# Gate one-hot rows for eight tokens at once, 72 candidate sums a head, and index look-ups in f16 in a decoder step with product-key experts

## The reference

```python
s1 = einsum('nhd,hkd->nhk', q[..., :half], sk[:, 0])      # 8 heads, 128 keys in each half
s2 = einsum('nhd,hkd->nhk', q[..., half:], sk[:, 1])
v1, i1 = top_k(s1, 16);  v2, i2 = top_k(s2, 16)
cand = (v1[..., :, None] + v2[..., None, :]).reshape(n, 8, 256)
cidx = (i1[..., :, None] * 128 + i2[..., None, :]).reshape(n, 8, 256)
sv, si = top_k(cand, 16)
e = take_along_axis(cidx, si);  g = softmax(sv)           # 128 experts and gates a token
y[n] = sum over hk of g[n, hk] * gelu(x[n] . u[e[n, hk]]) * v[e[n, hk]]
```

## Time and profile before

| | |
|---|---|
| time, median of 3 runs | 3537.03 us (3536.31 to 3539.16) |
| the profiled execution | 3537.08 us |
| span of its profile | 3535.3 us (1.8 us lie around it) |
| TensorE busy | 3286.6 us, 93% |
| VectorE busy | 2575.6 us, 73% |
| ScalarE busy | 1313.2 us, 37% |
| GpSimd busy | 1025.6 us, 29% |
| first and last matmul of `product` start | 1211.9 and 2428.0 us |

### The profile page before, as it was taken

How to read it: one execution, slowest core, us unless ns; L and a number is a source line. 1 busy time by engine, 2 the same in 40 slices (tenths; PEclk the granted TensorE clock), 3 DMA queues, 4 the chain that set the end, 5 groups by cost and what they waited for, 6 DMA issues and landing times. The chain is left out here.

```text
span 3535.3 us, 54538 instructions
## 1 busy us (share of the span) xinstructions
PE 3286.6 (93%) x20435; PEld 1984.8 (56%) x20435; DVE 2575.6 (73%) x5334; ACT 1313.2 (37%) x2581; POOL 1025.6 (29%) x1074
## 2 busy tenths in 40 slices
PE   7999988599889897999999999996999999999997
PEld 4668652366366554556565655653555555555554
DVE  4222651354423499999999999986888888888887
ACT  3000651221210123567767766662222222222222
POOL 0000000000000003699989988972111111111110
PEclk9999999788899998999999999998999999999998
DMA  3220875512422343878788787889878878888874
GB/s 144 95 95 31 310 280 217 188 72 105 182 64 76 115 178 131 248 256 280 271 286 286 271 290 258 282 294 405 303 284 303 293 285 296 299 288 294 296 285 153
DMA packets 213105, 803.41 MB, mean 227 GB/s; under 512 B 33825, under 2 KB 92321, under 8 KB 169089
## 3 DMA queue, kind: packets, MB, share of 16 engines
q1 hardware_dynamic: 176000, 531.81, 41.5%
q0 software_dynamic: 36864, 268.45, 21.7%
HBM read 665.19 MB, written 201.98 MB: 245 GB/s over the span
## 5 line engine op out<-in xcount | busy, mean ns | idle before, releaser
L1669 PE MATMUL psum<-arena 128*128 128x400 f16 x6144 | 1098.5, 337 | 45.4 <-DVE arena L1717 45.0
L2026 PE MATMUL psum<-arena 128*128 128x400 f16 x6144 | 1050.2, 332 | 26.9 <-DVE arena L2072 26.9
L2026 PEld LDWEIGHTS psum<-arena 128*128 128x128 f16 x6144 | 596.7, 97 | 480.4 <-DVE arena L2072 27.3
L1669 PEld LDWEIGHTS psum<-arena 128*128 128x128 f16 x6144 | 598.5, 99 | 474.1 <-DVE arena L1717 53.4
L1641 POOL TENSOR_SCALAR arena<-arena 128x128 f16<-128x128 f16 x800 | 711.9, 903 | 52.6 <-DVEq L1847 26.1
L116 POOL DMA_INDIRECT arena<-in_experts,arena x256 | 301.7, 1179 | 1180.8 <-DVE arena L149 1081.9
L135 ACT ACTIVATE arena<-arena 128x1 f32<-128x1 f32 x256 | 51.6, 202 | 920.2 <-DVE arena L128 920.1
L149 DVE SCALAR_TENSOR_TENSOR arena<-arena 128x1024 f32<-128x1024 f32 x256 | 330.9, 1293 | 21.3 <-ACT arena L139 5.2
L2079 DVE TENSOR_TENSOR arena<-arena,psum 128x800 f32<-128x800 f32 x256 | 252.0, 984 | 108.7 <-PE psum L2026 108.7
L128 DVE CUSTOM_DVE_ANT_0 arena<-arena 128x1024 f32<-128x1024 f32 x256 | 311.4, 1219 | 13.3 <-DMA arena<-in_experts,arena 12.3
L1898 ACT ACTIVATE arena<-arena 128x128 f16<-128x128 f16 x800 | 245.1, 388 | 89.2 <-DVE arena L1855 89.0
(11 more groups left out here) (230 smaller groups left out, 3569.2 us busy)
## 6 DMA issues: line engine op xcount, KB each, us to landing
arena<-in_u_feat SPq DMA_DIRECT2D x128, 512.0 KB, 6.8
arena<-in_experts SPq DMA_DIRECT2D x128, 512.0 KB, 5.4
scratch_acts<-arena SPq DMA_DIRECT2D x128, 400.0 KB, 4.4
arena<-scratch_gates SPq DMA_DIRECT2D x32, 1600.0 KB, 8.0
arena<-scratch_acts SPq DMA_DIRECT2D x128, 400.0 KB, 6.7
scratch_gates<-arena SPq DMA_DIRECT2D x48, 1024.0 KB, 6.7
out_k_win_sample<-in_cache_k SPq DMA_DIRECT2D x32, 1022.0 KB, 21.7
out_v_win_sample<-in_cache_v SPq DMA_DIRECT2D x32, 1022.0 KB, 21.7
```

The lines of the kernel that those rows point to most:

```text
L1669: last = pe.matmul(psum[:, 2 * p + k, 0:SLD], w[:, s, q, :], xs[:, q, k * SLD:(k + 1) * SLD], start=q == 0 and w is u_hi and xs is x_hi, s ...
L2026: last = pe.matmul(psum[:, 2 * (n % BANKS) + i, 0:SLD], w[:, s, k, q * P:(q + 1) * P], hs[:, s, k, i * SLD:(i + 1) * SLD], start=k == 0 an ...
```

## The change

- The one-hot rows of a unit are made for eight tokens at once with tokens innermost (`hots[partition, kind, key, token]`, f16): VectorE makes two instructions of 128x1024 (second index, then first index), both `is_equal` of a constant table `expert8` against the f16 indices of the eight tokens. GpSimd multiplies the second by the gate's high and low part, two `tensor_tensor` of 128x1024. ScalarE's `low_hots` is gone. The matmuls read single tokens out of this, so that both operands step by eight f16 elements.
- `copy_picks` is two copies and subtractions with f16 outputs instead of seven instructions.
- Of the 256 sums a head only 72 are made, in four blocks; `places_to_parts` finds the two parts of a place in them with some 14 small instructions in place of three.
- `one_hot` and `select_indices` work on f16 with the 16 candidates outermost; the two reductions become four additions of halves each (`collect`).
- At the stage's start GpSimd makes two tables of 1024 and 2048 elements in place of one of 128; VectorE waits for them.
- The semaphores follow: GpSimd's rows wait for VectorE's (`second_hots_ready`), TensorE waits for GpSimd's and VectorE's (`hots_ready`, `first_hots_ready`), VectorE also for GpSimd's rows of two units before.

```diff
+PAIR_BLOCKS = ((0, 2, 16, 0), (2, 2, 8, 32), (4, 4, 4, 48), (8, 8, 1, 64))
+NPAIR = 72
...
-            pool.iota(iota_i, pattern=[[1, P]], base=0, channel_multiplier=0).then_inc(iota_ready, 1)
-            pool.wait_ge(iota_ready, 1)
-            pool.tensor_copy(iota, iota_i).then_inc(iota_ready, 1)
-            pool.wait_ge(iota_ready, 2)
+            pool.iota(count8, pattern=[[1, P], [0, 8]], base=0, channel_multiplier=0).then_inc(iota_ready, 1)
+            pool.iota(count16, pattern=[[1, 16], [0, P]], base=0, channel_multiplier=0).then_inc(iota_ready, 1)
+            pool.wait_ge(iota_ready, 2)
+            pool.tensor_copy(expert8, count8).then_inc(iota_ready, 1)
+            pool.tensor_copy(j16, count16).then_inc(iota_ready, 1)
+            pool.wait_ge(iota_ready, 4)
...
-            def first_hots(unit):
+            def gate_hots(unit):
+                pool.wait_ge(second_hots_ready, unit["group"] // 2 + 1)
                 if unit["before"] > 0:
                     pool.wait_ge(gates_ready, unit["before"])
                 pool.wait_ge(picks_copied, order[unit["tile"]] + 1)
                 turned = turned_picks[:, order[unit["tile"]] % 2]
-                for i in range(4 * unit["groups"]):
...
-                    last = pool.tensor_scalar(hots[:, unit["buffer"], i, 0, :], iota, turned[:, 0, token:token + 1], None,
-                                              ALU.is_equal)
+                for k in range(2):
+                    some = turned[:, 2 + k, unit["token"]:unit["token"] + 8]
+                    last = pool.tensor_tensor(hots[:, unit["buffer"], 2 + k], hots[:, unit["buffer"], 1],
+                                              some.unsqueeze(1).broadcast_to([P, P, 8]), ALU.mult)
+                last.then_inc(hots_ready, 1)
...
-                pe.wait_ge(low_hots_ready, g + 1)
-                pe.wait_ge(first_hots_ready, g + 1)
+                pe.wait_ge(hots_ready, unit["group"] // 2 + 1)
+                pe.wait_ge(first_hots_ready, unit["group"] // 2 + 1)
...
-                        last = pe.matmul(psum[:, 6 + g % 2, i * PK:(i + 1) * PK], row[:, 1 + k, :], row[:, 0, :],
-                                         start=k == 0, stop=k == 1)
+                        last = pe.matmul(psum[:, 6 + g % 2, i * PK:(i + 1) * PK],
+                                         hots[:, unit["buffer"], 2 + k, :, 4 * j + i],
+                                         hots[:, unit["buffer"], 0, :, 4 * j + i], start=k == 0, stop=k == 1)
...
+                    for first, na, nb, c0 in PAIR_BLOCKS:
+                        dve.tensor_tensor(sums[r, :, c0:c0 + na * nb].rearrange("p h (a b) -> p h a b", a=na),
+                                          both[:, :, 0, first:first + na].unsqueeze(3).broadcast_to([rows, PH, na, nb]),
+                                          both[:, :, 1, 0:nb].unsqueeze(2).broadcast_to([rows, PH, na, nb]), ALU.add)
+                    dve.tensor_copy(idx16[r], idx[r].rearrange("p (h f) k -> p f k h", f=2))
...
+                    for k, shift in ((1, 4), (2, 3), (3, 2)):
+                        dve.tensor_scalar(places[r, k, :], places[r, 0, :], shift, None, ALU.logical_shift_right)
                     dve.drain()
+                    dve.tensor_copy(place[r], places[r])
                     dve.drain()
...
+                    dve.tensor_copy(parts16[r], parts[r].rearrange("p s (h k) -> p s k h", h=PH))
+                    dve.drain()
...
+                    dve.tensor_tensor((one_hot0, one_hot1)[k][r],
+                                      parts16[r, k].rearrange("p k h -> p (k h)").unsqueeze(1).broadcast_to([rows, 16, P]),
+                                      j16[r], ALU.is_equal)
...
+                    dve.tensor_tensor(o, o, idx16[r, k].unsqueeze(2).broadcast_to([rows, 16, 16, PH]), ALU.mult)
                     dve.drain()
+
+                def collect(k):
+                    o = (one_hot0, one_hot1)[k][r]
+                    for n in (8, 4, 2):
+                        dve.tensor_tensor(o[:, 0:n, :], o[:, 0:n, :], o[:, n:2 * n, :], ALU.add)
+                        dve.drain()
+                    dve.tensor_tensor(picks[r, k, :].rearrange("p (h k) -> p k h", h=PH),
+                                      o[:, 0, :].rearrange("p (k h) -> p k h", h=PH),
+                                      o[:, 1, :].rearrange("p (k h) -> p k h", h=PH), ALU.add)
...
                 if unit["before"] > 0:
                     dve.wait_ge(gates_ready, unit["before"])
+                    dve.wait_ge(hots_ready, unit["before"] // 2)
                 turned = turned_picks[:, order[unit["tile"]] % 2]
-                for i in range(4 * unit["groups"]):
...
-                    last = dve.tensor_scalar(hots[:, unit["buffer"], i, 1, :], iota, turned[:, 1, token:token + 1],
-                                             turned[:, 3, token:token + 1], ALU.is_equal, ALU.mult)
+                for k, ready in ((1, second_hots_ready), (0, first_hots_ready)):
+                    some = turned[:, k, unit["token"]:unit["token"] + 8]
+                    dve.tensor_tensor(hots[:, unit["buffer"], k], expert8,
+                                      some.unsqueeze(1).broadcast_to([P, P, 8]), ALU.is_equal).then_inc(ready, 1)
...
-            def low_hots(unit):
-                act.wait_ge(picks_copied, order[unit["tile"]] + 1)
...
-                for unit in units_at(n + 1):
-                    low_hots(unit)
```

More of the change, by code:

```diff
@@ L1648, in _ @@
                 for unit in units_at(n + 1):
-                    first_hots(unit)
+                    gate_hots(unit)
                 if TICKS[n]:
@@ new lines, in places_to_parts @@
+                    dve.drain()
+                    first, second = parts[r, 0, :], parts[r, 1, :]
+                    dve.scalar_tensor_tensor(out=first, in0=place[r, 2, :], scalar=-2.0, in1=place[r, 1, :],
+                                             op0=ALU.add, op1=ALU.max)
+                    dve.drain()
+                    dve.scalar_tensor_tensor(out=first, in0=place[r, 3, :], scalar=-8.0, in1=first,
+                                             op0=ALU.add, op1=ALU.max)
+                    dve.drain()
@@ new lines, in places_to_parts @@
+                    dve.scalar_tensor_tensor(out=first, in0=place[r, 0, :], scalar=-56.0, in1=first,
+                                             op0=ALU.add, op1=ALU.max)
+                    dve.drain()
+                    dve.tensor_scalar(bound[r, 0, :], first, 8.0, 16.0, ALU.mult, ALU.add)
+                    dve.tensor_scalar(bound[r, 1, :], first, 4.0, 32.0, ALU.mult, ALU.add)
+                    dve.drain()
+                    dve.tensor_tensor(bound[r, 0, :], bound[r, 0, :], bound[r, 1, :], ALU.min)
@@ new lines, in places_to_parts @@
+                    dve.drain()
+                    dve.scalar_tensor_tensor(out=bound[r, 0, :], in0=first, scalar=16.0, in1=bound[r, 0, :],
+                                             op0=ALU.mult, op1=ALU.min)
+                    dve.drain()
+                    dve.scalar_tensor_tensor(out=bound[r, 0, :], in0=first, scalar=56.0, in1=bound[r, 0, :],
+                                             op0=ALU.add, op1=ALU.min)
+                    dve.drain()
+                    dve.tensor_tensor(second, place[r, 0, :], bound[r, 0, :], ALU.subtract)
@@ L1794, in first_parts @@
                         dve.wait_ge(picks_turned, order[tile])
-                    dve.tensor_reduce(picks[r, 0, :], one_hot0[r], AX.X, ALU.add)
+                    collect(0)
                     dve.drain()
@@ L1800, in picks_and_gates @@
                     dve.tensor_reduce(den[r, 0, :], gate[r], AX.X, ALU.add)
-                    dve.tensor_reduce(picks[r, 1, :], one_hot1[r], AX.X, ALU.add)
+                    collect(1)
                     dve.drain().then_inc(top_used, 1)
@@ L1889, in high_part @@
                 act.mul(flat(u_hi[:, n % 3]), u[n % 3], W_SCALE).then_inc(hi_ready, 1)
-            def low_hots(unit):
-                act.wait_ge(picks_copied, order[unit["tile"]] + 1)
-                turned = turned_picks[:, order[unit["tile"]] % 2]
-                for i in range(4 * unit["groups"]):
-                    token = unit["token"] + i
-                    if i % 4 == 0:
-                        act.wait_ge(hots_ready, unit["group"] + i // 4 + 1)
-                    last = act.activation(hots[:, unit["buffer"], i, 2, :], hots[:, unit["buffer"], i, 1, :], ACT.Copy,
-                                          scale=turned[:, 4, token:token + 1])
-                    if i % 4 == 3:
-                        last.then_inc(low_hots_ready, 1)
             def copy_gates(unit):
```

75 lines of the change are left out of this document (26 added, 49 removed).

## The result

The changed kernel takes 3744.93 us (median of 4 runs, 3743.85 to 3747.09), the kernel before 3537.2 beside it: 1.0587 times as long (95% interval 1.0569 to 1.0606). The forecast was 3547 with a range to 3620, so the sign was right and the size far off.

A forecast was written before the change was run, and what follows sets the result against it. VectorE was taken to set the pace by a little, with TensorE right behind. 3537.08 - 30 (front) + 0.5 (start) + 95 x (9.91 - 9.49) (strided gate matmuls) = 3547.5; forecast 3547 us, range 3468 to 3620.

The forecast's parts named there:

- I take the ratio, twice the time: TensorE's strided gate matmuls: ScalarE's strided copy ratio, 1.9, taken over; a unit 1.80 us, a step 9.91 us.
- Rival D: Strided operands cost TensorE the full price of ScalarE's strided copy: 12.3 us a step, 3775 us; chance 0.07.
- break-even of 0.105 us a matmul: Gate matmul price at which gain and loss meet, 9.80 us a step.
- VectorE's own count: VectorE's busy time in a tile, summed by instruction: -25 us, from 147.5 to about 122.5.
- Rival C: VectorE's 16-bit two-input instructions run at the f32 rate; port's step about 10.4, 3610 us; chance 0.06.
- 5.5 + 2t a step: GpSimd's need in us a step, t being one product's price; with t 1.8 it is 9.1, below TensorE's 9.91.
- rival B: The port shared by GpSimd and VectorE is the bound: at t = 2.5 a step of 10.5, 3603 us; chance 0.15.
- The front: Steps 11 to 23, where two whole tiles are chosen: 30 of the 40 us lost come back.
- The start: GpSimd's larger tables at the stage's start delay VectorE's first low_part: +0.5 us (0 to 1.5).
- Queues: New waits between GpSimd's products and VectorE's rows: both have slack at 9.91 us a step, so no cost.
- Rival A: Strided operands cost TensorE nothing and t is near 1.8: 9.1 us a step, 3471 us; chance 0.30.
- A's variant with t = 2.0: Free strided operands, but each GpSimd product at 2.0 us: 9.5 us a step, 3508 us.

The follow-up runs named there:

- inner4: The changed kernel with tokens innermost in fours instead of eights, so both gate matmul operands step by 8 bytes instead of 16; 3564 us.
- inner2_low_scalar: inner2 with the second of GpSimd's two products of a unit, the low part, made by ScalarE token by token as before the change; 3470.4 us, ratio 0.9810.
- inner2: The changed kernel with tokens innermost in pairs instead of eights, so both gate matmul operands step by 4 bytes; 3506.2 us, ratio 0.9918.
- no_products: inner2 with ScalarE copying VectorE's one-hot row twice in place of both GpSimd products (gate table not right); 3465.3 us, one run.
- choice_only: The kernel before with only the change's choice part (72 sums, f16 look-ups, places worked back), rows made token by token as before; 3474.0 us, ratio 0.9814.

## Why the prediction was wrong

- **The step that failed: "I take the ratio, twice the time".** The bounds for a gate matmul were 0.056 and 0.264 us; I took 0.113 (1.80 / 16), and it was 0.231. By the steps that makes 95 x (11.86 - 9.91) = 185 of the 198 us that were missing. The nearest row was ScalarE's strided copy at 2.06 ns an element. I carried over its ratio to contiguous work on the same engine, 1.9. Its absolute price came nearer: TensorE's strided read came to 1.80 ns an element. TensorE takes a contiguous element in 0.44 ns (0.056 / 128), so this price is four times that of contiguous work. Rival D, to which I gave 0.07, used the absolute price; it overshot by 30 us (3775). That the two numbers lie close may be chance: no run shows that ScalarE's write and TensorE's read have the same limit.
- The break-even of 0.105 us a matmul was near: with the front's gain as measured in `inner4` (22.4 us) the same sum puts it at 9.72 a step, 0.101 a matmul, and `inner4` with 0.115 is slower than the kernel before beside it (3534.9) by 29 us.
- The Trainium skill's rule, SBUF — State Buffer (cachelines), had the direction. The equal price at steps of 16 and 32 bytes fits its lines of 16 bytes. Its condition for full rate, two accesses in a line, does not hold for this read: a step of 8 bytes has two and runs at half rate; a step of 4 bytes has four and runs at the full one.
- **VectorE's own count was nearly right, and hidden.** I had 147.5 - 25 = 122.5 us a tile; with no products beside it VectorE takes 120.9 (148.9 before in the same tile, so -28). An f16 instruction with two inputs takes 0.687 at 1024 (0.68 taken) and 1.22 at 2048 (1.21), a search of 72 0.218 and 0.223 against 0.406 and 0.411 at 256 (-0.19 each, as taken). Rival C is out.
- **What I left out of that sum: VectorE held by GpSimd.** My count of VectorE had no term for it; I put the conflict on GpSimd, as 5.5 + 2t a step, because the earlier trace rows show GpSimd held. One product alone took 2.27 us (all 100 in `inner2_low_scalar`), two in a row 4.12 where nothing held them, and I took 1.8 for each. VectorE is held too, 25 us a tile, which eats nearly the whole saving. The Trainium skill says so: by SBUF — State Buffer (Who interferes with whom) whoever starts first keeps the shared port for its whole instruction. I left that to rival B; the ends of lines 149 and 128 in the timelines above agree with it. In the changed kernel this costs next to nothing, as TensorE is busy throughout the tile; with the stride mended it is the difference between 3506 and 3465.
- **The front**: -30 taken, -21.7 measured. Four strided units cost 4 x 2.8 = 11 us of it, which I had not entered. But free strides alone do not bring that back (`inner2`: -22.8): there VectorE, held by the products, is late instead (step 20 takes 15.6 us, in `no_products` 12.0), and with no products the front is -27.5.
- **The start**: +0.5 taken. VectorE does wait 13.0 us at the start for the tables, but `product(0)` starts at 1211.65 against 1211.9, and step 11 0.9 us later. Queues cost nothing, as said: GpSimd's and VectorE's new waits lie beside a dense TensorE.
- Rival A was wrong on the strides; and with them free the kernel takes 3506, not 3471, for the port. A's variant with t = 2.0 had 3508, close by luck: it had GpSimd's turn at the port set the step, but what is short of time in `inner2` is VectorE, busy for 146.3 of 151.3 us a tile, and not GpSimd (99.9). Rival B's mechanism exists but is worth less than I put it: with strides out of the way the step is 9.41, not 10.5, and the loss sits in one late step a tile.

## What to carry to other kernels

An operand layout that suits the engine that writes it is paid for by the engine that reads it most: before elements are interleaved, count how many of them the reader finds in 16 bytes. When a price is taken from another engine's row, work out both its ratio and its absolute time of an element, and keep both as bounds: here the ratio was half of what was measured and the absolute time was near, which one case does not make a rule. And two engines that share an SBUF path are one resource: add a long GpSimd instruction with SBUF operands to VectorE's instructions with two inputs as well, not only to GpSimd's.

## What the runs showed of the hardware

- TensorE's moving f16 operand: 0.056 us a 128-column matmul at steps of 2 and 4 bytes, 0.115 at 8, 0.225 to 0.231 at 16 and 0.230 at 32. Weights at 16 bytes: load 148 ns instead of 98, which costs 0.01 us a step of 9.4.
- A GpSimd `tensor_tensor` of 1024 f16 takes 2.27 us, two in a row 4.12. Beside it VectorE's searches keep their 0.28 us, while instructions with two inputs are held until it ends: a sum of 128 elements took 1.98 us instead of 0.28 in the mean of four in `inner2`, a `tensor_tensor` of 2048 f16 2.9 instead of 1.22.
- GpSimd's 128-element `tensor_scalar` instructions (0.91 us in the mean in `choice_only`) hardly hold VectorE: line 149 is at 1.33 us there, against 1.28 in `no_products`.
